# Forming the first 2048 adaLN columns on TensorE, with x loaded first and modulated in place

## The reference

```python
c_act = jax.nn.silu(c)
mod = c_act @ ada_w[l] + ada_b[l]
sh1, sc1, g1, sh2, sc2, g2 = jnp.split(mod[:, None, :], 6, axis=-1)
z = rmsnorm(h, norm1_g[l]) * (1.0 + sc1) + sh1
proj = z @ w_in[l]
xa, ya, u, v = jnp.split(proj, [D_LRU, 2 * D_LRU, 2 * D_LRU + D_SGU], axis=-1)
o_lru = rg_lru_group(xa, jax.nn.gelu(ya), ...)
o_sgu = sgu_group(jax.nn.gelu(u), jax.nn.gelu(v), ...)
heads = jnp.concatenate([rmsnorm(o_lru, gnorm_lru_g[l]), rmsnorm(o_sgu, gnorm_sgu_g[l])], axis=-1)
h = h + g1 * (heads @ w_out[l])
z2 = rmsnorm(h, norm2_g[l]) * (1.0 + sc2) + sh2
h = h + g2 * moe(z2, ...)          # 32 experts, 4 chosen for a token
return rmsnorm(h, final_g)
```

## Time and profile before

| | |
|---|---|
| timed runs | 2080.45, 2081.16, 2083.56 us; median 2081.16 |
| profiled execution | 2070.52 us, of which span 2068.8 |
| mean granted TensorE clock | 0.979 of full |
| busy: PE, DVE, POOL, ACT | 1935.1, 996.9, 504.3, 352.7 us |
| moved by DMA | 527 MB, mean 255 GB/s |

### The profile page before, as it was taken

One profiled execution on the slowest core, in us unless ns is written; L12 is line 12 of the kernel. 1 busy time (PEld: TensorE's weight loads), 2 busy tenths in 40 slices (PEclk: granted clock), 3 DMA queues, 4 the chain that ended last, 5 costly groups with the idle time before them and its releaser, 6 DMA issues.

```text
span 2068.8 us, 53221 instructions
## 1 busy us (share of the span) xinstructions
PE 1935.1 (94%) x20256; PEld 804.0 (39%) x20257; DVE 996.9 (48%) x2268; ACT 352.7 (17%) x727; POOL 504.3 (24%) x536
## 2 busy tenths in 40 slices
PE   3999989978999999999999999999999999999994
PEld 3444444533333333334343343334333343344332
DVE  7656636354444435344444344444444454444434
ACT  3243221321110101111111111111111111110012
POOL 1100022132222222323232322333323233222221
PEclk9999999989999999999999999999999999999997
DMA  9233306332771864949596979889798797999975
GB/s 371 82 142 122 122 0 208 138 138 88 264 291 27 323 230 124 394 158 363 188 351 210 394 254 353 323 283 385 288 379 307 279 387 280 395 388 350 343 286 183
DMA packets 128956, 527.19 MB, mean 255 GB/s; under 512 B 17184, under 2 KB 47920, under 8 KB 79760
## 3 DMA queue, kind: packets, MB, share of 16 engines
q1 hardware_dynamic: 95152, 470.33, 58.7%
q0 software_dynamic: 33568, 56.29, 11.8%
q10 hardware_dynamic: 192, 0.06, 0.0%
HBM read 494.22 MB, written 32.38 MB: 255 GB/s over the span
## 4 chain that ended last, share of the span: by engine, by line
PE 80%; DMA 13%; DVE 3%; SPq 1%; issue 1%; ACT 1%; POOL 1%; DVEq 0%; ACTq 0%; POOLq 0%
PE psum L1210 40%; PE psum L1230 21%; DMA big<-in_exp_w_gu_dram 10%; PE psum L968 8%; PE psum L1127 5%; PE psum L1064 2%; DMA big<-in_exp_w_down_dram 2%; DVE gacc L1368 1%; PE psum L996 1%; PE psum L1171 1%; DVE r L1892 0%; SPq L491 0%; PE psum L985 0%; SPq L501 0%; DMA big<-in_w_out_dram 0%
## 5 line engine op out<-in xcount | busy, mean ns | idle before, releaser
L1210 PE MATMUL psum<-big,r 128*32 128x512 f32 x9152 | 1007.0, 598 | 34.0 <-DMA big<-in_exp_w_gu_dram 26.6
L1210 PEld LDWEIGHTS psum<-big,r 128*32 128x32 f32 x9152 | 290.9, 111 | 703.3 <-issue 648.7
L1230 PE MATMUL psum<-big,r 128*32 128x256 f32 x9152 | 512.0, 384 | 15.3 <-DVE r L1864 14.2
L693 POOL DMA_INDIRECT acc_rows<-r,scatter_idx x143 | 227.0, 1587 | 824.7 <-DVE r L1874 792.7
L1230 PEld LDWEIGHTS psum<-big,r 128*32 128x32 f32 x9152 | 295.3, 111 | 210.5 <-DVE r L1864 14.5
L879 ACT ACTIVATE r<-r,shift 128x128 f32<-128x128 f32 x376 | 154.2, 481 | 906.7 <-PE psum L1210 851.7
L1849 DVE TENSOR_TENSOR r<-psum,r 128x256 f32<-128x256 f32 x143 | 60.6, 424 | 362.3 <-PE psum L1210 359.6
L682 POOL DMA_INDIRECT r<-hs_rows,gather_idx x192 | 190.8, 994 | 86.4 <-issue 45.1
L1871 DVE TENSOR_TENSOR r<-psum,r 128x256 f32<-128x256 f32 x143 | 60.7, 425 | 279.8 <-PE psum L1230 279.8
L968 PE MATMUL psum<-r,big 128*128 128x512 f32 x384 | 166.3, 593 | 1.1 <-DVE r L1397 1.1
L1802 DVE STREAM_TRANSPOSE r<-r 128x1024 f32<-128x1024 f32 x47 | 97.8, 2082 | 108.8 <-issue 108.8
(11 more groups left out here) (278 smaller groups left out, 916.4 us busy)
## 6 DMA issues: line engine op xcount, KB each, us to landing
big<-in_exp_w_gu_dram SPq DMA_DIRECT2D x256, 1024.0 KB, 14.5
big<-in_exp_w_down_dram SPq DMA_DIRECT2D x128, 1024.0 KB, 20.5
big<-in_ada_w_dram SPq DMA_DIRECT2D x12, 2048.0 KB, 13.0
r<-in_x_dram SPq DMA_DIRECT2D x16, 512.0 KB, 12.8
big<-in_w_in_dram SPq DMA_DIRECT2D x4, 2048.0 KB, 19.7
r<-in_exp_b_gu_dram SPq DMA_DIRECT2D x128, 64.0 KB
big<-in_w_out_dram SPq DMA_DIRECT2D x2, 2048.0 KB, 13.6
hs_rows<-r POOLq DMA_DIRECT2D x8, 512.0 KB, 2.9
```

The costliest lines, as they stand in the source:

```text
L693: pool.indirect_dma_start(acc_quarters, bass.IndirectOffsetOnAxis(ap=scatter_idx[:, u:u + 1], axis=0), y_sb[:, u, :], None, bounds_check=4 ...
L1210: last = pe.matmul(psum[32 * j:32 * j + 32, u, :].rearrange("p (a n) -> p a n", a=2), izT[:, k, u * UNIT:(u + 1) * UNIT], rhs[:, :, 256 * ...
L1230: ins_ = pe.matmul(psum[32 * i:32 * i + 32, 4 + u % 2, 0:256], actT[:, u, f, :], down_slab(f)[:, 256 * i:256 * i + 256], start=(f == 0), s ...
```

## The change

SP loads the eight tiles of x first. Then it loads the first 2048 columns of ada_w not as four blocks of 512 columns but as four pairs of row tiles: pair j holds rows 256 j to 256 j + 255, all 2048 columns (`ada_pair`). GpSimd clears a tile `cact_cols` of eight blocks of 32 columns, and ACT puts silu(c) into the first column of each block. PE takes these 128x32 blocks as weights and the ada rows as moving data: for each of eight row tiles four matmuls of 512 columns, into the partition groups 0, 32, 64 and 96 of one bank. Row 32 i of the bank then holds columns 512 i to 512 i + 511 of the product. DVE copies the bank to `gacc`, and four small matmuls with columns 0, 32, 64 and 96 of the identity turn it into columns of `mod`.

The x tiles are still scaled by their row's reciprocal root, and turned before PE works on ada. ACT and DVE drain the banks with plain copies. Once `scale1` is there they go over `zT` again in place, ACT the even and DVE the odd tiles; each matmul of the first projection waits for its own tile. The softplus chain stands between the copies and the affine. GpSimd's loads wait for the first projection's bank instead of the last turned one.

```diff
 def bank_jobs():
     jobs = [("cols", 0, "dve")]
-    jobs += [("mod", j, "dve") for j in range(4)]
     jobs += [("zT", (k, th), "dve" if k % 2 else "act") for th in range(2) for k in range(KT)]
+    jobs += [("ada", 0, "dve"), ("mods", 0, "dve")]
...
+        def ada_pair(j):
+            return big[:, j, :].rearrange("p (k n) -> p k n", k=2)
...
+        cact_cols = r2[:, P:P + KT * UNIT].rearrange("p (k n) -> p k n", k=KT)
...
+            for t in range(TT):
+                sp_.dma_start(x_rows[:, t, :], x[t * P:(t + 1) * P, :]).then_inc(x_in[t], SEMW)
             for n, (kind, j) in enumerate(DENSE):
-                if n == DENSE_SLOTS:
-                    for t in range(TT):
-                        sp_.dma_start(x_rows[:, t, :], x[t * P:(t + 1) * P, :]).then_inc(x_in[t], SEMW)
+                if n < DENSE_SLOTS:
+                    sp_.dma_start(ada_pair(j), ada_w[2 * P * j:2 * P * (j + 1), 0:2048].rearrange("(k p) n -> p k n", p=P)
+                                  ).then_inc(dense_in[n], SEMW)
+                    continue
...
+            pool.memset(cact_cols, 0.0).then_inc(cact_spread, 1)
...
-            pool.wait_ge(filled, JOB[("zT", (KT - 1, 1))] + 1)
+            pool.wait_ge(filled, JOB[("xa", (0, 0))] + 1)
...
+            act.wait_ge(cact_spread, 1)
+            act.activation(cact_cols[:, :, 0], cols[:, ROW["c"]:ROW["c"] + 8], ACT.Silu).then_inc(cact_made, 1)
...
-            act.wait_ge(affine_made, 1)
             for th in range(2):
                 for k in range(0, KT, 2):
                     b = take("zT", (k, th))
-                    act.activation(zT[:, k, th * 512:(th + 1) * 512], b, ACT.Identity, bias=mod[:, SH1 + k:SH1 + k + 1],
-                                   scale=scale1[:, k:k + 1]).then_inc(act_drained, 1)
+                    act.activation(zT[:, k, th * 512:(th + 1) * 512], b, ACT.Copy).then_inc(act_drained, 1)
...
+            act.wait_ge(affine_made, 1)
+            act.wait_ge(act_drained, KT)
+            for th in range(2):
+                for k in range(0, KT, 2):
+                    z = zT[:, k, th * 512:(th + 1) * 512]
+                    act.activation(z, z, ACT.Identity, bias=mod[:, SH1 + k:SH1 + k + 1], scale=scale1[:, k:k + 1]
+                                   ).then_inc(z1_act, 1)
...
                 for k in range(KT):
+                    if (name, m) == ("xa", 0):
+                        pe.wait_ge(z1_dve if k % 2 else z1_act, 4 * th + k // 2 + 1)
...
-            for j in range(4):
-                mod_cols(j)
...
+            b = open_bank("ada", 0)
+            pe.wait_ge(cact_made, 2)
+            for n in range(4):
+                dense_ready(("ada", n))
+                for kk in range(2):
+                    k = 2 * n + kk
+                    for i in range(4):
+                        last = pe.matmul(b[32 * i:32 * i + 32, :], cact_cols[:, k, :], ada_pair(n)[:, kk, 512 * i:512 * i + 512],
+                                         start=(k == 0), stop=(k == KT - 1), skip_group_check=True)
+                last.then_inc(gemv_made if n < 3 else filled, 1)
+            b = open_bank("mods", 0)
+            wait_drained(pe, JOB[("ada", 0)])
+            for i in range(4):
+                last = pe.matmul(b[:, 4 * i:4 * i + 4], gacc[:, 0, i * P:(i + 1) * P], ident[:, 0:P:UNIT],
+                                 start=(i == 0), stop=True, skip_group_check=True)
+                if i == 0:
+                    last.then_inc(gemv_made, 1)
+            last.then_inc(filled, 1)
             dense_ready(("win", 0))
-            for who, drained in (("act", act_drained), ("dve", dve_drained)):
-                pe.wait_ge(drained, drained_before(JOB[("zT", (KT - 1, 1))], who))
...
-            mod_products(0)
...
-                modulate("zT", th, lambda k: zT[:, k, th * 512:(th + 1) * 512], scale1, SH1)
+                for k in range(1, KT, 2):
+                    b = take("zT", (k, th))
+                    dve.tensor_copy(zT[:, k, th * 512:(th + 1) * 512], b).then_inc(dve_drained, 1)
...
+            b = take("ada", 0)
+            dve.tensor_copy(gacc[:, 0, :], b).then_inc(dve_drained, 1)
+            b = take("mods", 0)
+            dve.tensor_tensor(mod[:, 0:16].rearrange("p (i b) -> p b i", b=4), b[:, 0:16].rearrange("p (b i) -> p b i", b=4),
+                              col("ada_b", 0, 16).rearrange("p (i b) -> p b i", b=4), ALU.add).then_inc(dve_drained, 1)
...
+            for th in range(2):
+                for k in range(1, KT, 2):
+                    z = zT[:, k, th * 512:(th + 1) * 512]
+                    dve.tensor_scalar(z, z, scale1[:, k:k + 1], mod[:, SH1 + k:SH1 + k + 1], ALU.mult, ALU.add
+                                      ).then_inc(z1_dve, 1)
```

More of the change, by code:

```diff
@@ L307, in build @@
         cact_made = sem("cact_made")
+        cact_spread = sem("cact_spread")
         ssum_made = sem("ssum_made")
@@ L310, in build @@
         x_scaled = sem("x_scaled")
+        z1_act = sem("z1_act")
+        z1_dve = sem("z1_dve")
         gemv_made = sem("gemv_made")
@@ L1361, in mod_products @@
                 dve.wait_ge(dense_in[n % DENSE_SLOTS], SEMW * (n // DENSE_SLOTS + 1))
-                if j >= 2:
+                if j >= 6:
                     dve.wait_ge(filled, JOB[gemv_job(j - 2)] + 1)
@@ L1377, in mod_add @@
                                   ).then_inc(dve_drained, 1)
-            dve.wait_ge(cact_made, 1)
-            mod_products(0)
[L1381 to L1397, removed]
-                                      ).then_inc(dve_drained, 1)
             for t in range(TT):
@@ L1423, in _ @@
             dve.tensor_scalar(sp[:, 7, :], sp[:, 5, :], -8.0, None, ALU.mult).then_inc(sp_made, 1)
+            b = take("ada", 0)
[3 more added lines that the diff above has]
+                              col("ada_b", 0, 16).rearrange("p (i b) -> p b i", b=4), ALU.add).then_inc(dve_drained, 1)
+            dve.wait_ge(dve_drained, drained_by(JOB[("mods", 0)])[1])
+            link(dve.tensor_scalar(scale1[:, :], mod[:, SC1:SC1 + 8], 1.0, None, ALU.add))
+            dve.tensor_tensor(scale1[:, :], scale1[:, :], col("norm1_g", 0, 8), ALU.mult).then_inc(affine_made, 1)
+            dve.wait_ge(affine_made, 1)
+            for th in range(2):
[3 more added lines that the diff above has]
+                                      ).then_inc(z1_dve, 1)
+            dve.wait_ge(cact_made, 2)
             def conv(ct):
```

## The result

Eight runs of the changed kernel have a median of 2072.41 us (2067.45 to 2075.96), eight of the kernel before 2082.18 (2076.44 to 2085.35). The ratio is 0.995, 95% interval 0.9939 to 0.9961: 9.8 us, 0.5%, faster. The forecast was 2073.0. In a second set of runs the changed kernel had 2071.35 us against 2082.29, ratio 0.9946 (0.9933 to 0.9959).

The account below looks back on a forecast made before the run. The prediction took PE's first projection start as the bound: 51.66 to 41.8 us, 9.9 us earlier, less 1.7 for a clock dip, gives 8.2, so 2081.16 becomes 2073.0 us timed. The range was 2068.5 to 2079.0.

Parts of the forecast that it names:

- Bound and method: Whole kernel: PE carries 80% of the span; the start of the first projection, 51.66 us in the profile, decides the effect.
- longer than 2017 us by more than the dip: Sign of being wrong: the stretch from first projection to end exceeds 2017 us by more than the clock loss.
- the dip: PE's clock falls to 1.2 GHz around the first projection, costing 1.7 us; the forecast with it had chance 0.48.
- Parameters: Start of kernel: the small parameter loads land 0.5 us later beside x; bounds 2.0 us earlier to 4.1 later.
- ACT, DVE and the turn: Before ada: squares start at about 12.7 us, the eighth scale ends at 26.0, PE's turn of x near 30.6.
- ada on PE: After the turn: 64 records at 0.110 us, 7.04 us in all; with at most 0.2 us for data, ending at 37.7.
- slower: Rival: the 32-wide ada matmuls do not overlap, taking 27.7 us instead of 7.0; time 2092; chance 0.03.
- From ada to z: Between ada and first projection: affine at 41.1 us, projection at 41.8, softplus hidden, w_in landing at 40.2 to 41.5.
- Clock: PE around the first projection: idle waits drop it to half rate, costing 1.7 us, bounds 0 and 3.4.
- No dip: Rival: small matmuls and short waits keep PE at 2.4 GHz; 9.9 us gained, 2071.3 us; chance 0.27.
- Sum: Whole kernel: 9.9 us earlier start less 1.7 for the clock, 8.2 us gained, 2073.0 timed.
- Given back: Rival: w_in or expert weight transfers set the pace, so an earlier start waits longer; 2077 to 2083 us; chance 0.08.

Follow-up runs that it names:

- the delay experiment: Twelve more throwaway matmuls of 512 columns ahead of the first projection, against the changed kernel with its PE waits filled by throwaway matmuls; 2082.40 us, 0.9996 of the kernel before.
- the matmuls alone: Against the kernel before: ada in row pairs on PE, still loaded ahead of x, x modulated leaving the banks, no second pass; 2071.70 us, ratio 0.9954.
- the filled kernel: The changed kernel with three throwaway matmuls in PE's two waits around the four small matmuls; 2070.73 us, then 2068.52 us in a second set.
- the one with the parameters first: The changed kernel, but SP waits for the parameter rows before it issues the x loads; one time, 2076.62 us.

## Why the prediction was right, point by point

**Bound and method.** Right: one instant, the start of the first projection, carries the effect, and the rest moves with it (the delay experiment, to 2 or 3 us). The weak step was to measure from a single profile. Its 51.66 was a quick draw (52.89 in the second), its expert stage 10 us shorter than in the second. For that reason the sign "longer than 2017 us by more than the dip" was no usable test: it came up in every later profile, from 2024.3 us (the matmuls alone) to 2033.0 (the changed kernel), and in the unedited kernel's second one too (2028.9).

**Parameters.** Taken 0.5 us later, measured 1.1 (10.70), and 0.9 to 1.5 in the later profiles of this and the filled kernel; inside the bounds of -2.0 and 4.1. The reason given, rows twice as large beside them, did not survive its test.

**ACT, DVE and the turn.** Squares from 13.1 (forecast 12.7), eighth tile scaled at 26.4 (26.0), turn ended at 30.7 (30.6). The end is right partly by luck. The forecast added eight banks at 0.54 or 0.55 us each behind the eighth tile. In fact PE was busy without a gap from 20.98, for 9.71 us or 0.61 a bank, so the turn hung on its own pace; the copies took only 0.60 us on ACT and 0.69 on DVE, and ACT waited 0.28 us for PE before each of its last four.

**ada on PE.** 7.05 us against 7.04, ending at 37.75 (37.7), no wait for data. The column groups overlap as in the earlier trace rows; the rival "slower" is out.

**From ada to z.** 3.5 us to the first tile against 4.1: the four small matmuls took 1.04 us and not the 1.87 of mod_cols, the copy 0.70. Against that the first tile in place came 1.0 us behind the affine (40.27 to 41.26), not 0.7. The start was 41.26 against 41.8. The softplus chain was through at 35.8, hidden. w_in landed at 40.4, at the early end of 40.2 to 41.5.

**Clock.** The term with the largest miss: 1.7 us taken, 2.7 lost in the first profile, none in the second. *No dip* was given 0.27 and the dip 0.48 as if the kernel decided it. It varies between executions of one kernel, so the timed median can be a mixture of both; the share of each in the timed runs is not known.

**Sum.** Forecast 9.9 - 1.7 = 8.2. From second profile to second profile of each kernel the start of v moved by 239.3 - 227.4 = 11.9 us and the span by 9.4; from first to first v moved by 7.8. Timed 9.8 and 10.9. The forecast is 1.6 and 2.7 us short of these. The quick start of the first profile (1.2 us) and a start 0.5 us earlier than forecast both point that way; the dip, 1.0 us larger in one execution and missing in the other, points both ways. That the time of the changed kernel came within 0.6 us of the forecast is in part luck: the scatter of the expert stage alone is larger. "Given back" is out for the head: all of the gain at v's start (7.8 us) is still there at 500 us (8.3), and a delay of 9.7 us comes through as 11.7. Whether 2 to 5 us of it go in the expert stage of this one kernel (1552 against 1547 us in its variants) the runs do not settle.

## What to carry to other kernels

When one engine is dense for most of a kernel, work out only when its dense work can start, and check that number by a delay of known length: here it passed through whole. Test each half of a change alone: moving a reduction from VectorE to 32-column matmuls brought nearly all of the gain, the reordered loads alone cost 0.4%, and together they come within 1 us of the pace of the DMA queue, behind which faster engines gained nothing here. Do not read the sign of a 0.5% effect from one profile of each kernel; compare stage by stage, and profile both kernels twice.

## What the runs showed of the hardware

- The granted clock after the same idle waits (0.91 and 1.62 to 1.63 us around four small matmuls) was 0.50 from 39.8 to 46.7 us in one execution, 5.4 us of it under the projection, and 1.00 in another of the same program. The variant with x in 2 KB rows, with the same two waits, had 0.50 from 42.5 to 45.9 us; the one with the parameters first had it from 39.2 us, in a wait of 3.36 us ahead of those two. The five profiles with matmuls in the waits had 1.00.
- The small parameter loads landed by 6.4 us with nothing beside them, at 9.6 beside ada pieces of 2 KB, at 10.5 to 11.6 beside x at the head of the queue in rows of 4 KB, at 10.6 with x in rows of 2 KB, and at 12.9 beside ada pairs of 8 KB. Row size alone does not order these.
- 16 loads of x in 2 KB rows moved 243 to 268 GB/s, 8 loads in 4 KB rows 313 to 400 (3 to 5 and 5 to 8 us of each profile with x at the head of the queue); ada blocks in 2 KB rows, 2 MB to a load, 381 to 399. Row size alone does not order these either.
- A granted clock that reads 1.00 near the start of a profile need not be the clock that PE had. The kernel with the matmuls alone turns x at a recorded 0.50 and then at 1.00; the kernel before (second profile) does the same turn with 1.00 in every window, and yet starts with the same few records:

```profile
33.00:35.00 2.00, 2.00 (x10) 0.50 1.03 386
38.00:40.00 2.00, 2.00 (x20) 1.00 1.05 389
...
42.00:44.00 2.00, 1.97 (x9) 1.00 1.05 385
48.00:50.00 2.00, 2.00 (x21) 1.00 1.05 385
```

  The slowest records agree as well: 476 ns at the recorded 0.50, 472 in the changed kernel's turn, where the window says 1.00, against 272 to 273 for the fast ones. So the slow first records of the turns were very probably run at the lower clock, and the quick 8.57 us of the earlier trace rows is a turn whose slow part was short. The four small matmuls fit this: 1.03 us in the changed kernel, 1.84 at a recorded 0.50, and 1.87 for mod_cols, which has the same form with one column and whose windows say 1.00.
